# Two token halves evacuated side by side, and mix matrices between the blocks, in a fused two-block transformer kernel

## The reference

```
# first block (one layer)
h = rms_norm(x, g_mix_pre);  proj = h @ w_in
merged = sigmoid(gate_a) * (attention @ w_attn_branch) + sigmoid(gate_b) * (hgrn @ w_hgrn_branch)
x = x + rms_norm(merged @ w_out, g_mix_post)
h = rms_norm(x, g_ffn_pre);  gate, up = split(h @ w_gate_up)
x = x + rms_norm((silu(gate) * up) @ w_down, g_ffn_post)
e = (p @ w_ple_proj) * sigmoid(rms_norm(x, g_ple_pre) @ w_ple_gate)
x = x + rms_norm(e, g_ple_post)
# second block, two layers
shift, scale, gate = split(silu(c) @ w_ada[l] + b_ada[l])
h = layernorm(x) * (1 + scale) + shift
u_f, z_f, cq, ckv, k_r, z_a = split(h @ w_in[l])
y_f = real(fft2(u_f)) @ w_fmix[l] * silu(z_f);   y_a = mla_attention(cq, ckv, k_r) * silu(z_a)
y = concat(y_f, y_a) @ w_out[l]
x = layernorm(4 ** 0.25 * x + gate * y, ln_g[l], ln_b[l])
```

## Time and profile before

| | us |
|---|---|
| median of 3 runs | 2385.9 (2381.72 to 2386.39) |
| the profiled execution's own time | 2390.88 |
| its span | 2389.1 |
| TensorE (PE) busy | 2246.1 (94%) |
| VectorE (DVE) busy | 1525.6 (64%) |
| ScalarE (ACT) busy | 1110.9 (46%) |
| GpSimd (POOL) busy | 74.2 (3%) |

### The profile page before, as it was taken

The page is one execution under the profiler, slowest core; times in us unless marked ns, Lnnn a source line. Parts: engine busy times, 40 slices in busy tenths (PEclk is TensorE's granted clock), DMA queues, the critical chain, the costliest instruction groups (busy, mean ns, idle before and its releaser), DMA issues.

```text
span 2389.1 us, 27085 instructions
## 1 busy us (share of the span) xinstructions
PE 2246.1 (94%) x10514; PEld 1864.6 (78%) x10514; DVE 1525.6 (64%) x1843; ACT 1110.9 (46%) x1549; POOL 74.2 (3%) x80
## 2 busy tenths in 40 slices
PE   8999999999988999999999999895999997799997
PEld 6788888887777788787887878674888876688876
DVE  5665476748767776676776777774365456445647
ACT  5565455443335444344433444555465444445532
POOL 1000000001100000000000001010000000000000
PEclk9999999999999999999999999897999998899999
DMA  6544654477886888888888887672464474344464
GB/s 223 177 132 138 193 162 154 135 240 265 272 273 211 287 283 282 281 290 283 279 283 285 295 282 253 211 258 86 133 185 132 135 248 144 107 135 138 150 221 140
DMA packets 233664, 500.64 MB, mean 210 GB/s; under 512 B 15696, under 2 KB 25600, under 8 KB 232128
## 3 DMA queue, kind: packets, MB, share of 16 engines
q1 hardware_dynamic: 229520, 485.64, 62.2%
q0 software_dynamic: 2416, 11.85, 1.4%
q10 hardware_dynamic: 1600, 1.43, 0.2%
HBM read 496.74 MB, written 2.12 MB: 209 GB/s over the span
## 4 chain that ended last, share of the span: by engine, by line
PE 60%; DMA 16%; DVE 11%; ACT 7%; issue 5%; POOL 1%; ACTq 0%; SPq 0%; DVEq 0%; POOLq 0%
PE bank L210 58%; DMA raw<-in_w_gate_up 5%; DMA raw<-in_w_down 4%; DVE wl L231 4%; DVE arena L239 4%; ACT wh L227 3%; PE bank L218 3%; DMA raw<-in_w_out 3%; ACT arena L227 2%; DVE arena L231 1%; DMA raw<-in_w_ple_gate 1%; DMA raw<-in_w_attn_branch 1%; DMA raw<-in_w_hgrn_branch 1%; ACT ah L227 1%; DMA arena<-in_w_fmix 1%
## 5 line engine op out<-in xcount | busy, mean ns | idle before, releaser
L231 DVE TENSOR_TENSOR wl<-raw,wh 128x1024 fp32r<-128x1024 f32 (+2 forms) x688 | 836.6, 1223 | 579.4 <-ACT wh L227 571.7
L227 ACT ACTIVATE wh<-raw 128x1024 fp32r<-128x1024 f32 (+2 forms) x688 | 716.6, 1048 | 898.5 <-PE bank L210 304.2
L210 PE MATMUL bank<-wh,hh 128*128 128x512 f32 (+1 forms) x1552 | 620.3, 400 | 37.2 <-DVE hl L231 16.3
L210 PE MATMUL bank<-wl,hh 128*128 128x512 f32 (+1 forms) x1552 | 606.7, 391 | 0.0
L210 PE MATMUL bank<-wh,hl 128*128 128x512 f32 (+1 forms) x1552 | 606.7, 391 | 0.0
L210 PE MATMUL bank<-wh,ah 128*128 128x512 f32 (+1 forms) x1200 | 472.1, 393 | 18.9 <-DVE wl L231 11.9
L210 PE MATMUL bank<-wh,al 128*128 128x512 f32 (+1 forms) x1200 | 466.8, 389 | 0.0
L210 PE MATMUL bank<-wl,ah 128*128 128x512 f32 (+1 forms) x1200 | 466.8, 389 | 0.0
L210 PEld LDWEIGHTS bank<-wh,hh 128*128 128x128 f32 x1552 | 296.5, 191 | 102.1 <-DVE hl L231 19.5
L210 PEld LDWEIGHTS bank<-wh,hl 128*128 128x128 f32 x1552 | 296.0, 191 | 61.4
L210 PEld LDWEIGHTS bank<-wl,hh 128*128 128x128 f32 x1552 | 296.8, 191 | 56.4
(11 more groups left out here) (115 smaller groups left out, 1119.5 us busy)
## 6 DMA issues: line engine op xcount, KB each, us to landing
raw<-in_w_in SPq DMA_DIRECT2D x264, 512.0 KB, 3.7
raw<-in_w_ada SPq DMA_DIRECT2D x192, 512.0 KB, 4.8
raw<-in_w_gate_up SPq DMA_DIRECT2D x176, 512.0 KB, 4.9
raw<-in_w_out SPq DMA_DIRECT2D x96, 512.0 KB, 5.2
raw<-in_w_down SPq DMA_DIRECT2D x88, 512.0 KB, 5.4
raw<-in_w_ple_gate SPq DMA_DIRECT2D x32, 512.0 KB, 5.1
raw<-in_w_attn_branch SPq DMA_DIRECT2D x16, 512.0 KB, 5.1
raw<-in_w_hgrn_branch SPq DMA_DIRECT2D x16, 512.0 KB, 5.0
```

Source lines behind the costliest of these rows:

```text
L210: return put("pe", lambda e: e.matmul(o, l, r, start=start, stop=stop_, skip_group_check=skip), w, sig, size(r) / 2400.0 * (4 if r.dtype = ...
L227: return e.activation(o, i, f, scale=scale, **k)
L231: return put(eng, lambda e: e.tensor_tensor(o, a, b, op), w, cost=vcost(eng, o))
```

## The change

The halves' evacuations go on `sides`; waits on keys keep the order between tasks (for instance `while 2 not in y_tok: yield`). Row moments of the layer norms come from sums that `scalar_tensor_tensor` puts out with `accum_out` (`stt_sum`) and from a Square with accumulator on ScalarE (`sq_sum`) in place of `bn_stats` and `bn_aggr`. `tr_half` gives two of its four scalings to VectorE. `prefetch` goes on GpSimd's queue for both layers, with places of their own for the two layers' constants (`CS_`, `CC_`, `WF_`), for layer 0 after the first `w_ple_gate` block; its products are issued by `mix_now` straight after the last block's matmuls. The products and sums on GpSimd go to VectorE. The operands are lent one block earlier, for 24 units, and `block` takes one weight unit a step, two at every third step, or until the unit at hand and two more are there. A "..." marks what is left out.

```diff
-            q = "pool" if l else "act"
+            q = "pool"
+            CS, CC, WF = CS_[l], CC_[l], WF_[l]
...
-            sides.append(mixes())
+            return mixes
...
-                while ptr[0] < len(stream) and slots and (n < 2 or len(unit_slot) <= g):
+                while ptr[0] < len(stream) and slots and (n < 1 + (at % 3 == 0) or len(unit_slot) <= g + 2):
...
-                    chain.append(evac(acc, t, done, 0, *args))
+                    sides.append(evac(acc, t, done, 0, *args))
...
-                chain.append(evac(acc, t, done, 1, *args))
+                sides.append(evac(acc, t, done, 1, *args))
...
-                    tm.append(act(T[:, q, :], ps[:, q, :], ACTF.Identity, t, tmp_rel.get(id(tmp)), scale=scale[q],
-                                  bias=bias[q]))
-                give(bk, tm[-1])
+                    if q < 2:
+                        t1 = act(T[:, q, :], ps[:, q, :], ACTF.Identity, t, tmp_rel.get(id(tmp)), scale=scale[q],
+                                 bias=bias[q])
+                    else:
+                        t2 = ts(T[:, q, :], ps[:, q, :], scale[q], bias[q], ALU.mult, ALU.add, t1,
+                                tmp_rel.get(id(tmp)))
+                tm = [t1, t2]
+                give(bk, t2)
...
-                t = tt(o, GB[n][:, m, :], o, ALU.add, t, hg_tok["ma", n], eng="pool")
+                t = tt(o, GB[n][:, m, :], o, ALU.add, t, hg_tok["ma", n])
...
-            block("wo", H, ALL, ev_post, n, t_row, borrow=last_of(Y, 16) if n == 2 else None)
+            block("wo", H, ALL, ev_post, n, t_row, borrow=last_of(Y, 24) if n == 1 else None)
...
         def ev_gate(acc, tok, done, c):
+            while "r" not in nx:
+                yield
...
-                    t1 = tt(YR[:, m, cs], YR[:, m, cs], GR[:, cs], ALU.mult, t, nx["row"],
-                            eng="dve" if n == 3 else "pool")
+                    t1 = tt(YR[:, m, cs], YR[:, m, cs], GR[:, cs], ALU.mult, t, nx["row"])
...
         def ev_pg(acc, tok, done, n):
...
+            if n == 0:
+                mixg[0] = prefetch(0, now(), mixd[0])
...
-            t = put("dve", lambda e: e.bn_aggr(MV[:, m, :], BNS[:, m, :, :].rearrange("p c s -> p (c s)")), t)
-            t = ts(VE[:, m:m + 1], MV[:, m, 1:2], EPS, None, ALU.add, None, t)
-            return tt(LR, VE[:, m:m + 1], CST[:, K_MH:K_MH + 1], ALU.pow, t, eng="pool")
+            ME, V = MV[:, m, :], VE[:, m:m + 1]
+            t = red(ME, SUMS[:, m, :, :], ALU.add, *t)
+            t = ts(ME, ME, 1.0 / D, None, ALU.mult, None, t)
+            t = tt(V, ME[:, 0:1], ME[:, 0:1], ALU.mult, t)
+            t = stt(V, ME[:, 1:2], EPS, V, ALU.add, ALU.subtract, t)
+            return tt(LR, V, CST[:, K_MH:K_MH + 1], ALU.pow, t, eng="pool")
+
+        def stt_sum(o, a, sc, b, op0, op1, acc_, *w):
+            return put("dve", lambda e: e.scalar_tensor_tensor(out=o, in0=a, scalar=sc, in1=b, op0=op0, op1=op1,
+                                                               accum_out=acc_), w, cost=vcost("dve", o))
...
+        def sq_sum(junk_, src, acc_, *w):
+            jk = (junk_.offset, size(junk_))
+            t = act(junk_, src, ACTF.Square, *w, jk_rel.get(jk), accum=acc_)
+            jk_rel[jk] = t
+            return t
...
             def norm(n):
...
+                if n < 4 and n not in tn and not tx_busy[n % 2]:
+                    tx_busy[n % 2] = True
+                    tn[n] = act(TX[n % 2], XR[:, m, n * 512:(n + 1) * 512], ACTF.Identity, t, rel, tx_rel.get(n % 2),
+                                scale=LR, bias=NM)
...
+        def mix_now(l):
+            g = mixg[l]()
+            while step(g):
+                step_all()
...
         def ev_pg_last(acc, tok, done, m):
+            while 2 not in y_tok:
+                yield
...
-                t = stt(XR[:, m, c2], YR[:, m, c2], r, XR[:, m, c2], ALU.mult, ALU.add, t_r, tks)
-                t = bn_stats(m, n, XR, t)
-                yield
-            if m:
-                prefetch(0, now(), mixd[0])
-            yield from pre_half(0, m, prel, t)
+                t = stt_sum(XR[:, m, c2], YR[:, m, c2], r, XR[:, m, c2], ALU.mult, ALU.add, SUMS[:, m, 0, n:n + 1],
+                            t_r, tks)
+                t2 = sq_sum(G[:, m, :], XR[:, m, c2], SUMS[:, m, 1, n:n + 1], t)
+                yield
+            yield from pre_half(0, m, prel, t, t2)
+            pre_done.append(0)
...
-            block("pgate", Y, ALL, ev_pg, n, borrow=last_of(H, 16) if n == 2 else None)
+            block("pgate", Y, ALL, ev_pg, n, borrow=last_of(H, 24) if n == 1 else None)
...
         block("pgate", Y, ALL, ev_pg_last, split="last")
+        mix_now(0)
...
             def begin():
+                while pre_done.count(l) < 2:
+                    yield
...
-                    prefetch(1, tk["za_done"], mixd[1])
+                    mixg[1] = prefetch(1, tk["za_done"], mixd[1])
...
-                    t1 = stt(XR[:, m, c2], Z[:, m, c2], LR, LB[:, c2], ALU.mult, ALU.add, t1, late["b"])
+                    t1 = stt_sum(XR[:, m, c2], Z[:, m, c2], LR, LB[:, c2], ALU.mult, ALU.add, SUMS[:, m, 0, n:n + 1],
+                                 t1, late["b"])
                     if l == 0:
-                        t1 = bn_stats(m, n, XR, t1)
+                        t2 = sq_sum(Z[:, m, c2], XR[:, m, c2], SUMS[:, m, 1, n:n + 1], t1)
...
-                block("wo2", Y, ALL, ev_o, n, borrow=last_of(H, 16) if n == 2 else None)
+                block("wo2", Y, ALL, ev_o, n, borrow=last_of(H, 24) if n == 1 else None)
             clear(H)
             block("wo2", Y, ALL, ev_o_last, split="last")
+            if l == 0:
+                mix_now(1)
```

More of the change, by code:

```diff
@@ L368, in idle @@
             until(lambda: not chain and not sides)
-        CS = kb(48, 4)[:, 0:2 * 258].rearrange("p (k n) -> p k n", k=2)
-        CC = kb(52, 1)
-        WF = kb(53, 4).rearrange("p (g n) -> p g n", g=8)
+        CS_ = [kb(o, 3)[:, 0:2 * 258].rearrange("p (k n) -> p k n", k=2) for o in (61, 48)]
+        CC_ = [kb(o, 1) for o in (60, 52)]
+        WF_ = [kb(o, 4).rearrange("p (g n) -> p g n", g=8) for o in (56, 53)]
         AB = kb(80, 8).rearrange("p (s g n) -> p s g n", s=2, g=8)
         def prefetch(l, rel, tk):
-            q = "pool" if l else "act"
+            q = "pool"
+            CS, CC, WF = CS_[l], CC_[l], WF_[l]
             dma(q, CS, A["k_cs"].rearrange("(k p) n -> p k n", p=P), f"fc{l}", [rel])
@@ L1416, in ev_post_last @@
                 return
+            while ("ta", 0) not in nx:
+                yield
             y_tok.clear()
@@ L1529, in program @@
         until(lambda: len(e_tok) == 4)
+        mixd = [{}, {}]
+        mixg = [None, None]
         def ev_pg(acc, tok, done, n):
@@ L1544, in ev_pg @@
             for m in range(2):
-                t = square_sum(YR[:, m, cs], SS[:, m, n:n + 1], t1)
+                t = act(G[:, m, :], YR[:, m, cs], ACTF.Square, t1, accum=SS[:, m, n:n + 1])
             for m in range(2):
-                t1 = tt(YR[:, m, cs], YR[:, m, cs], GR[:, cs], ALU.mult, t, t_row, eng="dve" if n == 3 else "pool")
+                t1 = tt(YR[:, m, cs], YR[:, m, cs], GR[:, cs], ALU.mult, t, t_row)
             y_tok[n] = [t, t1]
@@ L1572, in norm @@
             def norm(n):
-                tn[n] = act(TX[n % 2], XR[:, m, n * 512:(n + 1) * 512], ACTF.Identity, t, rel, tx_rel.get(n % 2),
-                            scale=LR, bias=NM)
-            norm(0)
+                if n < 4 and n not in tn and not tx_busy[n % 2]:
+                    tx_busy[n % 2] = True
+                    tn[n] = act(TX[n % 2], XR[:, m, n * 512:(n + 1) * 512], ACTF.Identity, t, rel, tx_rel.get(n % 2),
+                                scale=LR, bias=NM)
             for n in range(4):
-                if n < 3:
-                    norm(n + 1)
+                norm(n)
+                while n not in tn:
+                    yield
+                    norm(n)
+                norm(n + 1)
                 res = {}
@@ L1584, in pre_half @@
                 tx_rel[n % 2] = res["pe"]
-        mixd = [{}, {}]
+                tx_busy[n % 2] = False
+        pre_done = []
+        def mix_now(l):
+            g = mixg[l]()
+            while step(g):
+                step_all()
         def ev_pg_last(acc, tok, done, m):
+            while 2 not in y_tok:
+                yield
             prel, t_rp, t_row = nf["y_rd"], nf["r"], nf["row"]
@@ L1957, in ev_o @@
                 for m in range(2):
-                    t = stt(Z[:, m, cs], XR[:, m, cs], ALPHA, Z[:, m, cs], ALU.mult, ALU.add, t)
-                for m in range(2):
-                    t = put("dve", lambda e, m=m, n=n, cs=cs: e.bn_stats(BNS[:, m, n, :], Z[:, m, cs]), [t])
-                y_tk[n] = t
+                    t1 = stt_sum(Z[:, m, cs], XR[:, m, cs], ALPHA, Z[:, m, cs], ALU.mult, ALU.add,
+                                 SUMS[:, m, 0, n:n + 1], t)
```

(20 more changed lines are left out.)

8 lines of the change are left out of this document (6 added, 2 removed).

## The result

The changed kernel is slower: 2399.5 us median of 6 runs (2392.59 to 2402.82) against 2383.8 (2377.95 to 2387.04) for the kernel before beside it, a ratio of 1.0064 [1.0043, 1.0084], some 15 us. The profiled execution spans 2397.7 us, against 2389.1; the latter took 2390.9 us in all, 7 more than its kernel's median, so the two traces differ by less than the medians. The forecast was 2341.

A forecast was written before the change was run, and what follows sets the result against it. TensorE, 94% busy, was near its weight-stream limit from 800 to 1500, with two pauses at each layer boundary as the target. Terms 14 + 4.6 + 15 + 3 + 6 + 2 + 2 - 1 - 1 = 44.6 us gave 2341 us, range 2327 to 2366.

The forecast's parts named there:

- lending a block earlier and of the pacing: Operands lent one block earlier, one weight unit a step: neutral outside lent blocks, 0 us (between -3 and +3).
- 14 us: Boundary into layer 0: second pause goes, second pass starts at about 1647, not 1661; first pass kept at 16.5 us.
- 15 us: Boundary into layer 1: second pass starts at about 2030 instead of 2045.3, as half 1 is ready in time.
- the 4.6 and 3 behind it: Second passes shorter at full clock: 4.6 us at layer 0, 3 us at layer 1.
- the 2.3 of half 0's chain: Boundary into layer 0: half 0's chain 2.3 us shorter, first half starts at 1630.0 instead of 1632.29.
- lose up to about 9 us: Boundary into layer 0: half 1, run beside half 0's norms and splits, delayed by that much, ready by 1644.6.
- rival of lockstep: Half 1's operations issued among half 0's make half 0 8 us late at the layer boundaries; 2357 us, 17%.
- about even, 2013: Boundary into layer 1: half 0's chain loses five statistics, gains other operations; about even, start at 2013.
- GpSimd to VectorE: Twenty wide GpSimd operations become VectorE ones; only the last pair of branch sums counts, 2 us gained.
- the mixes and `w_fmix` at 6 us: Layer 1's mix matmuls move from mid-`w_out` to the boundary's pause, covered, with `w_fmix` loaded in time: 6 us gained.
- slower rival: Weight stream, 800 to 1600: pacing or added work holds raw slots longer; at 261 GB/s 2397 us, 5%.
- slow accumulations of the second rival: VectorE's accumulating form costs 0.69 us extra, not 0.15, at boundaries and tail: 12 us, 2353 us, 12%.

The follow-up runs named there:

- e1: Changed kernel with operands lent as before (at block 2, 16 units), new pacing kept: 2382.6 us, ratio 0.9997 to the kernel before.
- e4: Kernel before with only the earlier lending (24 units from block 1) and the new pacing rule: 2393.3 us, ratio 1.0041.
- e3: Changed kernel with late lending (block 2, 16 units) and the halves' evacuations one after the other on `chain`: 2387.1 us, ratio 1.0016 to the kernel before.
- e6: e1 with evacuations before the layers cut into finer turns, no wide operation issued in the turn of the other-engine one it awaits: 2371.9 us, ratio 0.9961.
- e12: Kernel before with only layer 1's mix products issued straight after the last `w_out` matmul of layer 0: 2376.7 us, ratio 0.9975.
- e10: e6 with both halves back on the `chain` list, one after the other: 2382.7 us, ratio 0.9995 to the kernel before.
- e8: e1 with all 20 wide sums and products on GpSimd again: 2378.7 us, ratio 0.9980 to the kernel before.
- e9: e6 with the 20 wide sums and products on GpSimd again, as in e8: 2365.1 us, ratio 0.9935 to the kernel before.

## Why the prediction was wrong

**The step that failed first** is the one that said of lending a block earlier and of the pacing that "it is neutral outside the lent blocks; inside, more splits are out ahead: 0 (between -3 and +3)". The working looked for what the rule does to the weight stream, and that is indeed unchanged. It did not ask what stands behind a split in its queue. Slots lent one block sooner, for 24 units and not 16, put splits whose loads are still under way in front of evacuations that TensorE waits for. That was 16 us (e1), shown from both sides (e4).

**The step that failed by most** is the pair "14 us" and "15 us", with the 4.6 and 3 behind it, 37 us in all, the 2.3 of half 0's chain among them. The second pause is gone at layer 1; at layer 0, 3.11 us of waiting are left in front of the second pass. But that the first pass "took 16.5 us" and "I keep that" was wrong: with half 1's operations among half 0's, both in order in the same two queues, the pass took 25.9 and 27.5 us, and no stretch to the end of the first block is shorter by over 0.1 us (59.4 to 61.4, 62.6 to 62.5). The pause was not removed but dealt out over the first pass. The second passes did get shorter, at clock 1.00: 15.8 us at layer 0 and 13.6 at layer 1, where they took 17.9 and 16.5; so 2.1 of the 4.6 us and 2.9 of the 3 came, and went again in the first pass. Nor did half 1 start with its results, as "Started at 1619.5" and the mark of 2 us had it: its first operation came 10.2 and 11.1 us after them. The worth of side by side is 3 to 4.5 us as built, and about 8 with finer turns.

The prediction had half 1 "lose up to about 9 us" to half 0, and charged half 0 nothing for half 1. Its rival of lockstep named the right mechanism, but in the wrong place. Its mark, a first matmul more than 22 to 25 us after half 0's results, was met with 27.0 and 31.7, yet it does not tell the two apart: the kernel before has 25.2 at layer 1, and e3, with the halves in turn, 25.2 and 29.7. Half 1 itself delays that matmul by only 2.4 and 2.0 us (e1, with 27.6 and 31.7, against e3); the rest it costs within the first pass, 25.9 and 27.5 us against 17.5 in e3. The rival's price, 16 us, was too low, as it counted half 1's work and not the waits that come with it: e6, which takes waits out and leaves the work, has passes of 18.4 and 20.7 us, with part of the second pause back.

**The chain of half 0.** At layer 1, "about even, 2013" is some 4.5 us too short: in turn, e3 has 29.7 us from half 0's results to the first matmul, the kernel before 25.2. From `w_out`'s end to that of the first block e3 needs 67.8 us and e12, which has the old statistics and the same place for the mixes, 61.8. It is not the added operations: e10 has them all and takes 61.9, with the first matmul after 23.8. It is their place in the turns. At layer 0 the 2.3 us did not come either. Up to the norm the chain is shorter, by 2.8 us in the kernel after and 2.5 in e3; but then the four mix copies (2.03 us) and two weight splits (2.01) stand on ScalarE between the norm and the first scalings, and in e3 the first matmul comes 25.2 us after the results, not 21.4. The prediction left the splits "where they are", in front of the norm, where the earlier trace rows has them; here two of them moved behind it.

**GpSimd to VectorE**, 2 us to the good, has the wrong sign: about 4 us to the bad (e8; intervals that just overlap, but e9 against e6 and the starts of `w_out` say the same). I priced one pair at the end of the branch stretch by its duration alone.

What was right: the mixes and `w_fmix` at 6 us (e12, interval 2 to 10); side by side into the gate blocks, 2 us in the forecast, 3.3 in the traces of e1 and e3; the weight stream at 285 GB/s against the slower rival's 261. The slow accumulations of the second rival did not come. VectorE's timeline of the kernel after:

```profile
1634.26 0.74 DVE L1583 SCALAR_TENSOR_TENSOR arena<-arena,st 128x512 f32<-128x512 f32 x1
1634.93 0.08 DVE L1583 DVE_READ_ACCUMULATOR arena<-arena,st 128x1 f32 x1
1634.93 0.75 DVE L1583 SCALAR_TENSOR_TENSOR arena<-arena,st 128x512 f32<-128x512 f32 x1
```

The accumulating form takes 0.75 us, as the plain one in the earlier trace rows, and the next one starts 0.67 us after it, the 0.08 us read of the accumulator included. The Trainium skill (Vector Engine (DVE) Microarchitecture Reference, Points that are easy to get wrong) has this form at half its throughput; the trace does not show that here.

Put together, in differences of the ratio times 2384 us: lending +16, GpSimd +4, the mixes -6, the turns of half 0's chain at layer 1 +6 (from the traces), side by side -4.5. That is +15.5, and +15.3 was measured. The terms come from different kernels, so part of how well it closes is luck.

Open are the worth of the pacing rule, what the mix copies cost on ScalarE net of the place of the products, and the two terms of 1 us, for the constants' load and the tail, which no run took apart. Lending early with evacuations put ahead of the splits was not tried.

## What to carry to other kernels

In an in-order queue the depth of prefetch is a latency for everything issued behind it: before lending more buffers, look at which operation stands behind the last prefetched one, and who waits for it. Two tasks side by side gain more if no operation is issued in the same turn as the one of another engine that it waits for (8 us here, against 3 to 4.5); otherwise a wait of one becomes a wait of both, and a removed pause comes back in pieces within the pass behind it. So a pause should be costed to the end of the next pass, not to its own end.

## What the runs showed of the hardware

`scalar_tensor_tensor` with an accumulator costs VectorE nothing over the plain form (0.75 us on 128x512 fp32, with a read of 0.08 us), where ScalarE's read takes 0.19. But at the end of the chain VectorE waits 0.87 us between its last sum and the reduce, while ScalarE does the last Square and reads its accumulator; the `bn_stats` that it replaces stays on VectorE:

```profile
1975.55 0.08 DVE L1583 DVE_READ_ACCUMULATOR arena<-arena 128x1 f32 x1
1976.49 0.16 DVE L248 TENSOR_REDUCE st<-st 128x2 f32<-128x8 f32 x1 [0.87 <-ACT arena L227]
```

This is e6, half 0 into layer 1. Giving two of four scalings from PSUM to VectorE brought nothing either: the kernel lets VectorE's pair wait for ScalarE's (`t1` in the diff), so the two engines take the bank one after the other, ScalarE's pair in 0.81 us and VectorE's in 0.73, and the group is no shorter than four on ScalarE (from the first transpose to the matmul it feeds 4.2 us in e6, 4.1 before).
